# A fused transformer kernel on Trainium2: a halved first weight chunk, splits moved between the input's rows, a shorter last norm, and GpSimd's rows behind a later count

## The chip, the cores and the metric

One core of one Trainium2 chip runs the whole program. Its engines are TensorE (PE; its weight loads are shown as PEld), VectorE (DVE), ScalarE (ACT), GpSimd (POOL) and SyncE (SP, which here only issues DMAs). They run side by side and wait for each other on counting semaphores. The metric is the device time of one execution in microseconds (us). Three runs of the kernel before took 1221.53, 1223.04 and 1223.50 us, so its median is 1223.04 us.

## The reference

The input is one sequence of 256 tokens by 1024 features in float32. Three norm, attention and feed-forward (FFN) stages follow each other; all matrix products are float32.

```
h = layer_norm(x, g, b)
for l in range(2):                                   # first block
    proj = h @ w_in[l]                               # q, k, v, u
    a = diff_attention(q, k, v, lam, lam_init, subln_g[l])
    f = real(fft(fft(u, features), tokens)) per group, @ w_f[l] + b_f[l]
    h = layer_norm(ALPHA * h + concat(a, f) @ w_o[l], ln1_g[l], ln1_b[l])
    h = layer_norm(ALPHA * h + (silu(h @ w_g) * (h @ w_u)) @ w_down, ln2_g[l], ln2_b[l])
mod = silu(c) @ w_ada + b_ada                        # second block: shifts, scales, gates
u = modulate(rmsnorm(h), mod);  h += 0.5 * gate * swiglu(u)
u = modulate(rmsnorm(h), mod);  h += gate * mixer(u)   # stick-breaking attention and conv
u = modulate(rmsnorm(h), mod);  h += 0.5 * gate * swiglu(u)
return rmsnorm(h)
```

## The kernel before, in words

**Chunks.** All weights come as one stream of 184 chunks of 128 x 2048 float32 (1 MB each). SP loads chunk j into `raw[j % 3]`. ACT rounds it to the short matmul type (`w_hi`, a copy), DVE takes the rest (`w_lo = raw - w_hi`), and PE multiplies in passes: high by high, high by low, low by high. The inputs are split in the same way: ACT writes a scaled and shifted tile `x_full` from the transposed norm, and DVE makes `x_hi` and `x_lo` of it (`input_split`, eight tiles of 128 features, two instructions each).

**Order and waits.** Every engine's program is written out by hand and runs in order. The counts that matter: `hi_ready` (ACT has rounded a chunk), `lo_ready` (DVE has its rest; SP may also load that buffer again), `chunk_done` (PE is through with it), `x_ready` (input tiles split), `z_ready` (quarters of the normalised rows `z`). Before ACT rounds chunk j it waits until PE is through with chunk j - 3.

**Layers.** A layer of the first block takes 45 chunks: V0, V1, U0, U1, Q0, K0, Q1, K1, four for the output projection, 33 for the FFN. V0 and U0 use the input tiles 0 to 3, V1 and U1 the tiles 4 to 7 (`token_projection`, L466 on). Between V1 and U0 PE makes tables from `wf` and the constants `c32` (`fourier_tables`, L618) and waits there for both to land. The FFN's first two chunks, 12 and 13 of a layer, use all eight tiles each.

**A norm.** DVE adds the residual banks to `h` (L1191), takes statistics (L1178, L1181, L1184), GpSimd raises to the power of -1/2 (L349), DVE writes `z = (h - mean) * root` (L1200), PE transposes `z` (L519), ACT writes `x_full` (L837), DVE splits it. The product `h = z * gain + shift` that the next residual needs is done by GpSimd (`residual_stream`, L364 and L369, eight instructions), behind the input's split. Behind the last of the five layer norms DVE does it itself (L1469, L1473), since the next norm reads its result at once: ACT squares and sums `h` (L847), DVE and GpSimd make the root (L1217, L349) and DVE scales (L1226).

**The program's first microseconds.** SP issues four loads of `x`, then chunks 0 and 1, the constants, chunk 2. ACT's own DMA queue brings the first constants, `lp` and `wf` for both layers. GpSimd's queue brings `cp`, and once chunk 1 has landed two `gain_rows` and three `gate_rows` of 512 KB each. In the DMA rows q1 is SP's queue, q10 is ACT's, q0 is GpSimd's.

## Time and profile before

| | us |
|---|---|
| median of three runs | 1223.04 |
| the profiled execution, its own time | 1223.15 |
| its span, first to last instruction | 1221.4 |
| PE busy | 1161.7 (95%) |
| DVE busy | 869.0 (71%) |
| ACT busy | 606.9 (50%) |
| GpSimd busy | 115.8 (9%) |

What lies around the span is 1.75 us. Busy times overlap, so they don't add to the span. The timeline lists instructions in order of time, and the idle time ahead of one on its engine stands behind it in brackets with what ended it. The busy time of a matmul includes its drain, which overlaps the next one: what counts is the distance between starts.

### The profile page before, as it was taken

To read this page: it belongs to the slowest core of one execution; us is meant where nothing else is said; L and a number is where in the kernel's file an instruction comes from. 1 tells how busy PE (TensorE), PEld (TensorE's weight loads), DVE (VectorE), ACT (ScalarE), POOL (GpSimd) and SP (SyncE) were. 2 spreads that over 40 slices of the span, in tenths; PEclk is the share of its full clock that TensorE was granted. 3 is DMA by queue.
4 is the path that set the end of the run, shared out by engine and by line. 5 is a ranking of instruction groups with operands and counts; after the bars stand their busy time and mean duration, and the time that the engine had idled before them with its cause. 6 is when DMAs were issued, how large, how long until landed. Compare 5 with 4: busy or idle time off the path is not lost.

```text
span 1221.4 us, 17674 instructions
## 1 busy us (share of the span) xinstructions
PE 1161.7 (95%) x6612; PEld 998.8 (82%) x6612; DVE 869.0 (71%) x1128; ACT 606.9 (50%) x738; POOL 115.8 (9%) x99
## 2 busy tenths in 40 slices
PE   5999999999899999999969999999999998999997
PEld 4887888888687788888858888877989997888886
DVE  6486968888858586888886788877468377555555
ACT  4473644444458364444444445444695445444443
POOL 3301700000330170000010000000000000000000
PEclk9999999999999999999979999998999999999999
DMA  9612577775362257777535667753423543555540
GB/s 360 233 70 104 180 257 302 276 292 207 114 229 70 104 184 256 299 279 294 203 135 210 241 258 272 291 192 150 166 97 139 188 158 145 208 197 174 200 175 35
DMA packets 34847, 242.62 MB, mean 199 GB/s; under 512 B 3792, under 2 KB 5216, under 8 KB 8176
## 3 DMA queue, kind: packets, MB, share of 16 engines
q1 hardware_dynamic: 27792, 196.03, 43.2%
q0 software_dynamic: 5520, 45.17, 10.1%
q10 hardware_dynamic: 1488, 0.76, 0.2%
q8 instruction: 33, 0.54, 0.2%
q14 instruction: 14, 0.11, 0.0%
HBM read 240.90 MB, written 1.05 MB: 198 GB/s over the span
## 4 chain that ended last, share of the span: by engine, by line
PE 78%; DVE 11%; ACT 5%; issue 4%; DMA 1%; POOL 0%; SPq 0%; DVEq 0%; ACTq 0%
PE bank L429 38%; PE bank L462 24%; PE bank L464 12%; ACT w_hi L829 2%; DVE x_parts L1235 1%; DVE w_lo L1162 1%; DVE work L1286 1%; PE bank L608 1%; DVE small L1178 1%; DMA raw<-stream 1%; PE bank L519 1%; DVE h L1191 1%; DVE x_parts L1233 1%; DVE h L1211 1%; PE bank L585 1%
## 5 line engine op out<-in xcount | busy, mean ns | idle before, releaser
L1162 DVE TENSOR_TENSOR w_lo<-raw,w_hi 128x2048 fp32r<-128x2048 f32 x184 | 430.1, 2342 | 148.1 <-ACT w_hi L829 147.8
L462 PE MATMUL bank<-x_parts,w_hi 128*128 128x512 f32 x1408 | 499.1, 398 | 5.3 <-DVE w_lo L1162 3.3
L464 PE MATMUL bank<-x_parts,w_lo 128*128 128x256 f32 x1408 | 395.1, 281 | 0.0
L829 ACT ACTIVATE w_hi<-raw 128x2048 fp32r<-128x2048 f32 x184 | 350.7, 1907 | 47.7 <-PE bank L429 41.6
L462 PEld LDWEIGHTS bank<-x_parts,w_hi 128*128 128x128 f32 x1408 | 264.6, 188 | 72.4 <-DVE w_lo L1162 4.6
L464 PEld LDWEIGHTS bank<-x_parts,w_lo 128*128 128x128 f32 x1408 | 266.0, 189 | 1.4
L429 PE MATMUL bank<-x_parts,w_hi 128*128 128x256 f32 x832 | 153.0, 286 | 0.7 <-ACT work L1078 0.7
L429 PE MATMUL bank<-w_hi,hid_hi 128*128 128x512 f32 x352 | 139.3, 396 | 2.8 <-DVE hid_lo L1274 2.8
L429 PE MATMUL bank<-w_lo,hid_hi 128*128 128x512 f32 x352 | 139.0, 395 | 0.0
L429 PE MATMUL bank<-w_hi,hid_lo 128*128 128x512 f32 x352 | 138.8, 394 | 0.0
L429 PEld LDWEIGHTS bank<-x_parts,w_hi 128*128 128x128 f32 x832 | 129.4, 191 | 3.8 <-issue 2.0
L429 PE MATMUL bank<-x_parts,w_lo 128*128 128x256 f32 x416 | 117.6, 283 | 0.0
L1286 DVE SCALAR_TENSOR_TENSOR work<-work,c_act 128x384 f32 x168 | 104.0, 619 | 5.9
L869 ACT ACTIVATE hid_hi<-work 128x512 fp32r<-128x512 f32 x44 | 27.8, 632 | 127.7 <-PE bank L429 114.7
L853 ACT ACTIVATE work<-bank 128x512 f32<-128x512 f32 x44 | 26.3, 597 | 122.6 <-PE bank L464 122.6
L429 PEld LDWEIGHTS bank<-w_hi,hid_hi 128*128 128x128 f32 x352 | 66.0, 187 | 20.1 <-DVE hid_lo L1274 4.1
L429 PE MATMUL bank<-w_hi,x_parts 128*128 128x512 f32 x224 | 74.1, 408 | 6.4 <-DVE x_parts L1235 4.5
L429 PEld LDWEIGHTS bank<-x_parts,w_lo 128*128 128x128 f32 x416 | 79.6, 191 | 0.0
L429 PEld LDWEIGHTS bank<-w_hi,hid_lo 128*128 128x128 f32 x352 | 66.0, 187 | 16.0
L429 PEld LDWEIGHTS bank<-w_lo,hid_hi 128*128 128x128 f32 x352 | 66.0, 188 | 14.1
L1274 DVE TENSOR_TENSOR hid_lo<-work,hid_hi 128x512 fp32r<-128x512 f32 x44 | 32.7, 743 | 60.1 <-ACT hid_hi L869 60.1
L349 POOL TENSOR_TENSOR small<-small 128x1 f32<-128x1 f32 x18 | 11.6, 643 | 540.3 <-DVE small L1217 426.0
(168 smaller groups left out, 1227.8 us busy)
## 6 DMA issues: line engine op xcount, KB each, us to landing
raw<-stream SPq DMA_DIRECT2D x184, 1024.0 KB, 4.8
work<-ada POOLq DMA_DIRECT2D x24, 1536.0 KB, 7.1
gain_rows<-rows POOLq DMA_DIRECT2D x11, 512.0 KB, 4.9
gate_rows<-rows POOLq DMA_DIRECT2D x3, 512.0 KB, 11.1
h<-x SPq DMA_DIRECT2D x4, 256.0 KB, 5.0
out<-z SPq DMA_DIRECT2D x4, 256.0 KB, 2.1
c<-consts SPq DMA_DIRECT2D x1, 962.0 KB, 12.9
wf<-w_f ACTq DMA_DIRECT2D x2, 256.0 KB, 14.5
```

Of the source, the lines that this page charges most:

```text
L429: last = nc.tensor.matmul(out, stationary, moving, start=start and i == 0, stop=stop and i == 2, skip_group_check=True)
L462: nc.tensor.matmul(pair[:, n, :], wh[:, k, cols], x_parts[:, k, :, :].rearrange("p a n -> p (a n)"), start=k == 0, stop=False, skip_group_ ...
L464: last = nc.tensor.matmul(pair[:, n, 0:S], wl[:, k, cols], x_hi[:, k, :], start=False, stop=k == KT - 1, skip_group_check=True)
L519: last = nc.tensor.transpose(XT[k // 2][:, k % 2 * S + m * P:k % 2 * S + (m + 1) * P], z[:, m, k * P:(k + 1) * P], ident)
L585: last = nc.tensor.matmul(SCORES[u][:, m * S:(m + 1) * S], qT[r:r + HD, p, m * P:(m + 1) * P], kT[r:r + HD, p, :], start=True, stop=True, ...
L608: last = nc.tensor.matmul(bank[:, at:at + VD], aT_s[:, h % 2, kk, m * P:(m + 1) * P], v_s[:, kk, h * VD:(h + 1) * VD], start=kk == 0, stop ...
L829: nc.scalar.activation(w_hi[j % SLOTS][:, :], raw[j % SLOTS][:, :], ACT.Copy).then_inc(hi_ready, 1)
L853: nc.scalar.activation(gate_rest.rearrange("p (a n) -> p a n", a=2), GATE[:, :, S:2 * S], ACT.Copy)\
L869: nc.scalar.activation(out[:, :, :].rearrange("p k n -> p (k n)"), hidden, ACT.Copy)\
L1162: nc.vector.tensor_tensor(w_lo[j % SLOTS][:, :], raw[j % SLOTS][:, :], w_hi[j % SLOTS][:, :].bitcast(F32), ALU.subtract).then_inc(lo_ready, 1)
L1274: nc.vector.tensor_tensor(lo[:, :, :].rearrange("p k n -> p (k n)"), hidden, hi[:, :, :].rearrange("p k n -> p (k n)").bitcast(F32), ALU.s ...
L1286: nc.vector.scalar_tensor_tensor(acc, ada_raw[:, k, :], c_act[:, k:k + 1], acc, ALU.mult, ALU.add).then_inc(ada_step, 1)
```

## The change

- At the start SP loads chunk 0 as two halves of 1024 columns, ACT rounds and DVE subtracts each half by itself, and `wf` is loaded from SP's queue, after chunk 2 and ahead of the constants.
- In the first chunks of a layer, and of the mixer, the split of chunk 1 stands between the input tiles 0 to 3 and 4 to 7 on DVE; on ACT it does so in layer 0.
- Ahead of each FFN of the first block, DVE subtracts the first half of chunk 13 before the input's tiles and the second half after them.
- The last layer norm's rows come from two operations a quarter, `y = (h - mean) * gain` and `h = y * root + shift`, and they stand between the residual sums of rows 0 and 1.
- GpSimd's rows wait also for `lo_ready`: four chunks of the layer in the first case, chunk 14's in the second.
- PE runs 30 matmuls on a tile of ones before anything else.

```diff
 SP
-            for s in range(SLOTS):
+            sp.dma_start(raw[0][:, 0:CH // 2], stream[0, :, 0:CH // 2]).then_inc(first_half_landed, 16)
+            sp.dma_start(raw[0][:, CH // 2:], stream[0, :, CH // 2:]).then_inc(raw_landed[0], 16)
+            for s in range(1, SLOTS):
                 sp.dma_start(raw[s][:, :], stream[s]).then_inc(raw_landed[s], 16)
-                if s == 1:
-                    sp.dma_start(c32[:, TRI:], consts32[:, TRI:]).then_inc(consts_landed, 16)
+            for l in range(DEPTH):
+                sp.dma_start(wf[l][:, :, :], w_f[l].rearrange("g c d -> c g d")).then_inc(wf_landed, 16)
+            sp.dma_start(c32[:, TRI:], consts32[:, TRI:]).then_inc(consts_landed, 16)
 GpSimd
-            def residual_stream(n):
+            def residual_stream(n, chunks):
                 pool.wait_ge(gain_rows_landed, 32 * n + 32)
                 pool.wait_ge(x_ready, 8 * n + 8)
+                pool.wait_ge(lo_ready, chunks)
                 pool.wait_ge(z_ready, 4 * n + 4)
...
-                residual_stream(2 * l)
+                residual_stream(2 * l, 3 * LT * l + 4)
...
-                residual_stream(2 * l + 1)
+                residual_stream(2 * l + 1, 3 * LT * l + G0 + 3)
 PE
+            def warm_up(count):
+                pe.wait_ge(ones_ready, 1)
+                for _ in range(count):
+                    nc.tensor.matmul(B[0][:, 0:P], ones_r[:, :], ones_r[:, :], start=True, stop=True,
+                                     skip_group_check=True)
+            warm_up(30)
 ACT
                 act.dma_start(lp[l][:, :], layer_params[l]).then_inc(params_landed, 16)
-                act.dma_start(wf[l][:, :, :], w_f[l].rearrange("g c d -> c g d")).then_inc(wf_landed, 16)
...
-            split(0, 0, first=True)
-            split(0, 1, first=True)
-            act.wait_ge(params_landed, 16 * DEPTH)
+            act.wait_ge(first_half_landed, 16)
+            nc.scalar.activation(w_hi[0][:, 0:CH // 2], raw[0][:, 0:CH // 2], ACT.Copy).then_inc(first_half_hi, 1)
+            act.wait_ge(raw_landed[0], 16)
+            nc.scalar.activation(w_hi[0][:, CH // 2:], raw[0][:, CH // 2:], ACT.Copy).then_inc(hi_ready, 1)
...
+                input_full(2 * l, *columns, range(0, KT // 2))
+                if l == 0:
+                    split(t, 1, first=True)
+                input_full(2 * l, *columns, range(KT // 2, KT))
                 split(t, 2, first=l == 0)
+                act.wait_ge(params_landed, 16 * DEPTH)
                 split(t, 3)
 DVE
-                input_split(2 * l)
+                input_split(2 * l, range(0, KT // 2))
                 split(t, 1)
+                input_split(2 * l, range(KT // 2, KT))
                 split(t, 2)
                 split(t, 3)
...
+                split_half(t, 13, 0)
                 input_split(2 * l + 1)
-                split(t, 13)
+                split_half(t, 13, 1)
...
-            layer_scaled(4)
+            def last_rows(m):
+                for b in (2 * m, 2 * m + 1):
+                    nc.vector.scalar_tensor_tensor(tile_of(z, b), tile_of(h, b), moments[:, m, 0:1],
+                                                   gain_rows[:, 0, b % 2 * HALF:(b % 2 + 1) * HALF], ALU.subtract,
+                                                   ALU.mult).then_inc(y_ready, 1)
+                dve.wait_ge(inv_root_ready, 2 * 4 + m + 1)
+                for b in (2 * m, 2 * m + 1):
+                    dve.wait_ge(y_ready, b + 1)
+                    nc.vector.scalar_tensor_tensor(tile_of(h, b), tile_of(z, b), inv_root[:, m:m + 1],
+                                                   gain_rows[:, 1, b % 2 * HALF:(b % 2 + 1) * HALF], ALU.mult,
+                                                   ALU.add).then_inc(h_ready, 1)
...
+            layer_residual(4, LAYER_CHUNKS * DEPTH, (0, 1))
+            last_rows(0)
+            layer_residual(4, LAYER_CHUNKS * DEPTH, (2, 3))
+            last_rows(1)
```

The order of instructions at three places, of before and of the change. First SP's queue from the program's start; `h<-x` are the four loads of the input, `raw0` to `raw2` the chunk buffers, `c32` the constants. Before:

```order
L318 DMA h<-x 128x512 x4
L322 DMA raw0<-stream 128x2048
L322 DMA raw1<-stream 128x2048
L324 DMA c32<-consts32 128x1924
L322 DMA raw2<-stream 128x2048
```

With the change:

```order
L321 DMA h<-x 128x512 x4
L324 DMA raw0<-stream 128x1024
L325 DMA raw0<-stream 128x1024
L327 DMA raw1<-stream 128x2048
L327 DMA raw2<-stream 128x2048
L329 DMA wf0<-w_f 128x4x128
L329 DMA wf1<-w_f 128x4x128
L330 DMA c32<-consts32 128x1924
```

The constants have moved from third among the big loads to last, behind chunk 2 and both `wf`, which came from ACT's queue; chunk 3, the next load, stays behind all of them.

Second, DVE at the input of layer 0 (the same in layer 1), around the split of chunk 1, `w_lo1<-raw1,w_hi1`. Before, the last of eight input tiles and what follows it:

```order
L1233 CAST x_parts<-x_full 128x256 [waits x_full_ready]
L1235 TENSOR_TENSOR x_parts<-x_full,x_parts 128x256 [waits x_hi_ready]
L1162 TENSOR_TENSOR w_lo1<-raw1,w_hi1 128x2048 [waits hi_ready]
L1162 TENSOR_TENSOR w_lo2<-raw2,w_hi2 128x2048 [waits hi_ready]
L1162 TENSOR_TENSOR w_lo0<-raw0,w_hi0 128x2048 [waits hi_ready]
```

With the change, the fourth tile, the chunk and the fifth tile:

```order
L1262 CAST x_parts<-x_full 128x256 [waits x_full_ready]
L1264 TENSOR_TENSOR x_parts<-x_full,x_parts 128x256 [waits x_hi_ready]
L1182 TENSOR_TENSOR w_lo1<-raw1,w_hi1 128x2048 [waits hi_ready]
L1262 CAST x_parts<-x_full 128x256 [waits x_full_ready]
L1264 TENSOR_TENSOR x_parts<-x_full,x_parts 128x256 [waits x_hi_ready]
```

Chunk 1 has moved ahead of eight of the sixteen instructions of the input.

Third, DVE behind the last layer norm, from the statistics of rows 0's second half on. Before:

```order
L1181 BN_AGGR small<-small 128x2 [waits bn_done]
L1184 TENSOR_SCALAR small<-small 128x1 [waits moments_ready]
L1200 TENSOR_SCALAR z<-h,small 128x512 [waits inv_root_ready] x4
L1469 TENSOR_TENSOR h<-z,gain_rows 128x512 [waits z_ready,gain_rows_landed]
L1469 TENSOR_TENSOR h<-z,gain_rows 128x512 [waits z_ready] x3
L1473 TENSOR_TENSOR h<-h,gain_rows 128x512 [waits h_scaled] x4
L1217 TENSOR_SCALAR small<-small 128x1 [waits squares_done]
```

With the change:

```order
L1213 TENSOR_SCALAR small<-small 128x1 [waits moments_ready]
L1506 SCALAR_TENSOR_TENSOR z<-h,small,gain_rows 128x512 x2
L1512 SCALAR_TENSOR_TENSOR h<-z,small,gain_rows 128x512 [waits y_ready,inv_root_ready]
L1512 SCALAR_TENSOR_TENSOR h<-z,small,gain_rows 128x512 [waits y_ready]
L1220 SCALAR_TENSOR_TENSOR h<-h,bank 128x512 [waits res_bank,h_ready]
L1207 BN_STATS small<-h 128x6 [waits summed]
```

Twelve instructions on quarters of `h` have become eight, four for each row block; those of block 0 stand ahead of the residual sums of block 1.

## Rows read from the trace of the kernel before

**Rows 1.** The page, part 4: the chain that ended last, shares by engine.
```profile
PE 78%; DVE 11%; ACT 5%; issue 4%; DMA 1%; POOL 0%; SPq 0%; DVEq 0%; ACTq 0%
```

**Rows 2.** Windows: stretch, length, busy us (count) of PE, PEld, DVE, ACT, POOL, clock, DMA, GB/s.
```profile
18.00:21.00 3.00, 3.00 (x8) 2.32 (x9) 2.86 (x10) 2.90 (x6) 0.00 (x0) 1.00 1.02 409
125.00:312.00 187.00, 184.77 (x963) 155.88 (x963) 150.52 (x156) 90.33 (x83) 26.49 (x18) 1.00 0.67 253
617.00:636.00 19.00, 9.27 (x58) 8.35 (x57) 16.43 (x37) 4.25 (x12) 3.68 (x6) 0.65 0.25 78
```

**Rows 3.** Timeline of layer 0's input: start, us, engine, instruction [idle before, releaser].
```profile
8.64 0.69 DVE L1178 BATCH_NORM_STATS2 small<-h 128x6 f32<-128x512 f32 x1 [0.26 <-DMA h<-x]
...
9.73 2.08 DVE L1200 TENSOR_SCALAR z<-h,small 128x512 f32<-128x512 f32 x4
...
11.78 1.91 ACT L829 ACTIVATE w_hi<-raw 128x2048 fp32r<-128x2048 f32 x1 [5.30 <-DMA raw<-stream]
13.72 2.29 DVE L1162 TENSOR_TENSOR w_lo<-raw,w_hi 128x2048 fp32r<-128x2048 f32 x1 [1.91 <-ACT w_hi L829]
14.50 1.91 ACT L829 ACTIVATE w_hi<-raw 128x2048 fp32r<-128x2048 f32 x1 [0.81 <-DMA raw<-stream]
...
16.32 3.98 ACT L837 ACTIVATE x_full<-bank,cp 128x256 f32<-128x256 f32 x8
...
17.80 0.77 PE L429 MATMUL bank<-w_hi,x_parts 128*128 128x512 f32 x1 [3.72 <-DVE x_parts L1235]
...
25.57 1.92 ACT L829 ACTIVATE w_hi<-raw 128x2048 fp32r<-128x2048 f32 x1 [3.47 <-PE bank L429]
...
29.92 1.30 DVE L1351 TENSOR_TENSOR work<-lp 128x64 f32<-128x64 f32 x1
...
30.75 1.88 PE L618 MATMUL bank<-wf,c 128*128 128x512 f32 x4
...
43.59 1.09 ACT L940 ACTIVATE work<-bank 128x512 f32<-128x512 f32 x2 [3.46 <-PE bank L429]
```

**Rows 4.** DMA queues from 17 to 20 us: packets, MB, share of 16 engines.
```profile
DMA packets 342, 1.23 MB, mean 409 GB/s; under 512 B 35, under 2 KB 137, under 8 KB 260
...
q1 hardware_dynamic: 98, 0.67, 54.4%
q0 software_dynamic: 128, 0.50, 41.8%
q10 hardware_dynamic: 116, 0.05, 6.4%
```

**Rows 5.** Line L923, the two loads of wf: from issue to landing.
```profile
DMA to landing us min/median/max: 7.9/14.5/21.1
```

**Rows 6.** Timeline of layer 1's input.
```profile
327.59 8.88 DVE L1162 TENSOR_TENSOR w_lo<-raw,w_hi 128x2048 fp32r<-128x2048 f32 x3
...
329.93 0.50 PE L429 MATMUL bank<-w_hi,x_parts 128*128 128x512 f32 x1 [1.05 <-DVE w_lo L1162]
```

**Rows 7.** Timeline of the input of layer 0's FFN, and of layer 1's (last row).
```profile
123.50 0.29 DVE L1233 CAST x_parts<-x_full 128x256 fp32r<-128x256 f32 x1 [1.35 <-ACT x_full L837]
...
128.82 5.58 DVE L1162 TENSOR_TENSOR w_lo<-raw,w_hi 128x2048 fp32r<-128x2048 f32 x2
...
131.16 0.50 PE L462 MATMUL bank<-x_parts,w_hi 128*128 128x512 f32 x1 [0.87 <-DVE w_lo L1162]
...
435.80 0.51 PE L462 MATMUL bank<-x_parts,w_hi 128*128 128x512 f32 x1 [0.87 <-DVE w_lo L1162]
```

**Rows 8.** Timeline of the last layer norm's rows on DVE.
```profile
623.61 2.07 DVE L1200 TENSOR_SCALAR z<-h,small 128x512 f32<-128x512 f32 x4
...
625.60 2.49 DVE L1469 TENSOR_TENSOR h<-z,gain_rows 128x512 f32<-128x512 f32 x4
...
628.00 2.49 DVE L1473 TENSOR_TENSOR h<-h,gain_rows 128x512 f32<-128x512 f32 x4
```

**Rows 9.** Timeline of DVE's last instructions.
```profile
1216.05 1.42 DVE L1621 SCALAR_TENSOR_TENSOR z<-h,small,gain_rows 128x512 f32<-128x512 f32 x2
```

More of the change, by code:

```diff
@@ L198, in fused_blocks @@
         common_landed = sem("common_landed")
+        first_half_landed = sem("first_half_landed")
+        first_half_hi = sem("first_half_hi")
         x_landed = [sem(f"x_landed{b}") for b in range(4)]
@@ L225, in fused_blocks @@
         inv_root_ready = sem("inv_root_ready")
+        y_ready = sem("y_ready")
         z_ready = sem("z_ready")
@@ L516, in transposes @@
                     m, c = b // 2, b % 2
-                    pe.wait_ge(z_ready, 4 * n + b + 1)
+                    pe.wait_ge(z_ready, 4 * back(n) + b + 1)
                     for k in range(4 * c, 4 * c + 4):
@@ L829, in split, with input_full @@
                 nc.scalar.activation(w_hi[j % SLOTS][:, :], raw[j % SLOTS][:, :], ACT.Copy).then_inc(hi_ready, 1)
-            def input_full(n, gain, shift):
-                for k in range(KT):
+            def input_full(n, gain, shift, ks=range(KT)):
+                for k in ks:
                     act.wait_ge(transposed, 4 * back(n) + k // 2 + 1)
@@ L1002, in _ @@
                 if l == 0:
-                    input_full(0, lambda k: cp[:, LNI_G + k:LNI_G + k + 1], lambda k: cp[:, LNI_B + k:LNI_B + k + 1])
+                    columns = (lambda k: cp[:, LNI_G + k:LNI_G + k + 1], lambda k: cp[:, LNI_B + k:LNI_B + k + 1])
                 else:
-                    input_full(2 * l, *layer_columns(l - 1, LN2_G, LN2_B))
+                    columns = layer_columns(l - 1, LN2_G, LN2_B)
+                    split(t, 1)
+                input_full(2 * l, *columns, range(0, KT // 2))
+                if l == 0:
+                    split(t, 1, first=True)
+                input_full(2 * l, *columns, range(KT // 2, KT))
                 split(t, 2, first=l == 0)
+                act.wait_ge(params_landed, 16 * DEPTH)
                 split(t, 3)
@@ L1163, in split, with split_half @@
                                         w_hi[j % SLOTS][:, :].bitcast(F32), ALU.subtract).then_inc(lo_ready, 1)
+            def split_half(t, j, part):
+                cols = slice(part * (CH // 2), (part + 1) * (CH // 2))
+                dve.wait_ge(hi_ready, 3 * t + (j + 1))
+                last = nc.vector.tensor_tensor(w_lo[j % SLOTS][:, cols], raw[j % SLOTS][:, cols],
+                                               w_hi[j % SLOTS][:, cols].bitcast(F32), ALU.subtract)
+                if part == 1:
+                    last.then_inc(lo_ready, 1)
             def tile_of(buffer, b):
@@ L1185, in layer_stats, with layer_residual @@
                         .then_inc(spread_ready, 1)
-            def layer_residual(n, chunks):
+            def layer_residual(n, chunks, banks=range(4)):
                 dve.wait_ge(h_ready, 4 * n)
-                for b in range(4):
+                for b in banks:
                     bank_summed(n, b, chunks)
@@ L1227, in rms_scaled, with input_split @@
                                             ALU.mult, ALU.mult).then_inc(z_ready, 1)
-            def input_split(n):
-                for k in range(KT):
+            def input_split(n, ks=range(KT)):
+                for k in ks:
                     at = 8 * back(n) + k + 1
@@ L1332, in _ @@
                 layer_stats(0, b)
-            dve.wait_ge(common_landed, 16)
-            dve.wait_ge(c_act_ready, 1)
             for l in range(DEPTH):
@@ L1340, in _ @@
                 if l == 0:
-                    split(0, 0)
+                    dve.wait_ge(first_half_hi, 1)
+                    nc.vector.tensor_tensor(w_lo[0][:, 0:CH // 2], raw[0][:, 0:CH // 2],
+                                            w_hi[0][:, 0:CH // 2].bitcast(F32), ALU.subtract)
+                    dve.wait_ge(hi_ready, 1)
+                    nc.vector.tensor_tensor(w_lo[0][:, CH // 2:], raw[0][:, CH // 2:],
+                                            w_hi[0][:, CH // 2:].bitcast(F32), ALU.subtract).then_inc(lo_ready, 1)
                 else:
                     keep_shifts(l - 1)
-                input_split(2 * l)
+                input_split(2 * l, range(0, KT // 2))
                 split(t, 1)
+                input_split(2 * l, range(KT // 2, KT))
                 split(t, 2)
                 split(t, 3)
+                dve.wait_ge(common_landed, 16)
+                dve.wait_ge(c_act_ready, 1)
                 dve.wait_ge(params_landed, 16 * DEPTH)
@@ L1484, in _ @@
             keep_shifts(2)
-            input_split(6)
+            input_split(6, range(0, KT // 2))
             split(MIX_T, 1)
+            input_split(6, range(KT // 2, KT))
             t = MIX_T
```

14 lines of the change are left out of this document (3 added, 11 removed).

## The prediction, made before the changed kernel was run

> **What bounds the kernel now.** I read the chain that ended last first: PE holds 78% of it [rows 1], and inside an FFN, from 125 to 312 us, PE is busy 184.8 of 187.0 us [rows 2]. So time is to be had only where PE waits or runs at the lower clock: at the joints, where a norm hands over to the next input. Then I read the timeline at those joints, and at the start the DMA queues. The reader should see four things. At the start PE's first product begins at 17.80 us [rows 3]: chunk 0 was landed at 11.7, chunk 1 at 14.5, and ACT, in order, rounds both before it turns to the input at 16.32. Ahead of layer 1's second chunk PE waits 1.05 us for DVE's `w_lo` [rows 6]. Ahead of each FFN's second chunk it waits 0.87 us for the same [rows 7]. And behind the last layer norm DVE's three passes over four quarters hold everything up [rows 8].
>
> **The start.** Durations from rows 3: a rounding of 1.91 us halves to 0.96, a subtraction of 2.29 to 1.15. The eight input tiles take 5.3 us on DVE (123.50 to 128.82 [rows 7]), 0.66 each. A chunk on PE takes 5.45 us: chunks 2 and 3 lie between 32.63 (30.75 + 1.88) and 43.6.
>
> Step 1, DMA. `wf` is 1024 packets of 512 B. A packet of ACT's queue costs 26 ns of one engine (6.4% of 48 engine-us by 116 [rows 4]). The two loads landed 7.9 and 21.1 us after their issue [rows 5], so I estimate that some 430 of the packets had gone when `x` was complete and 640 when chunk 0 was: 0.7 and 1.0 us over 16 engines. Without them `x` is complete at 7.9 us, chunk 0 at 10.7, its first half (0.52 MB at 0.41 MB a us [rows 4]) at 9.5, chunk 1 at 13.4.
>
> Step 2, ACT and DVE. `z` is done at 11.81 - 0.7 = 11.1. ACT rounds the halves by 10.5 and 11.7 and goes on to the input. DVE subtracts from 11.1 to 13.4, splits the first tile by 14.1, and PE starts at 14.1, 3.7 us sooner. Chunk 1, now behind ACT's first four tiles, is rounded by about 15.7; DVE has four tiles by 16.0, chunk 1 by 18.3, tiles 4 to 7 by 21.0. PE asks for chunk 1 at 19.6 and then for a tile every 1.4 us: no wait. Before, chunk 0 lasted 7.7 us (17.80 to 25.5), because matmuls stood 0.375 us apart (8 in 3.00 us [rows 2], against 0.23 at the full rate), although the record of the granted clock says 1.00 there. With the full clock PE is through chunk 1 at 25.0.
>
> Step 3, what that meets. Then come the Fourier tables, which want `wf` and the constants. These now stand behind chunk 2 in SP's queue, and chunk 3 behind them, while GpSimd's five loads of 512 KB run beside (issued once chunk 1 is landed, as before). From 17 to 20 us the three queues got 98, 128 and 116 packets, nearly one for one, whatever their size [rows 4]. So the 64 small packets an engine of `wf` each wait for one of GpSimd's 40 of 4 KB, which cost 157 ns (41.8% of 48 by 128). Chunk 2 lands at 15.9 (13.4 + 1.05 MB at 0.41); then 40 x 157 + 64 x 26 ns = 8.0 us to 23.9; the constants (0.98 MB) 26.3; chunk 3 28.9. PE waits 1.3 us for the constants, makes the tables by 28.2 and has chunk 2 by 33.7. Chunk 3 is rounded and subtracted by 33.1, in time; PE is through it at 39.1. But ACT now waits, behind chunk 3, for DVE's lambda (1.3 us [rows 3] and about 0.4 behind it), copies V (1.0, two of the pair at 43.59), rounds chunk 4 (1.9), and DVE subtracts beside GpSimd (2.5, my estimate between 2.29 and the 2.79 of rows 7): 40.2. PE starts chunk 4 at 40.3 instead of 43.6. **Gain 3.3 us**: PE's own path was worth more, 5.9 (3.7 and 2.2 of clock). All later work of the layer shifts with it. The ends I keep: 5.9 if the transfers keep up, 1.0 if chunk 3 lands 2.3 us later still.
>
> In the Trainium skill, "DMA: Bandwidth & Descriptors", section "Queues, rings and completion order", a DMA engine goes round its queues packet by packet, not byte by byte. By it `wf` is a bad neighbour for GpSimd's rows, as worked out above; the counts of rows 4 agree. Were bytes shared evenly, `wf` and the constants (1.5 MB at 0.2) would be landed at 23.3, there would be no wait at the tables, and the start would give about 4.
>
> The 30 warm-up matmuls (128 x 128, short type, on ones) are in no row. From the nearest, 0.375 us for 512 columns at the lower rate, I bound one between a quarter of that and all of it: 2.8 to 11.3 us from 1.1 us on, so the end is at 3.9 to 12.4. `z`'s first quarter is there at 9.0, so the late end delays the transposes by up to 3.4 us and PE's start by perhaps 2; an early end leaves some 5 us of idleness in which the clock can fall again, and chunk 0 costs up to 2.2 more. Either way PE is through chunk 1 by 27.2 and loses at most 0.9 to the wait above. I take 0.
>
> **Layer 1's input.** DVE takes chunk 1 behind four tiles: ready at 327.59 - 2.65 + 2.29 = 327.2, while PE is through chunk 0 at 328.7; tile 4 is split at 327.9. The wait of 1.05 us goes, with the slower first matmul behind it (0.16): **1.2 us**. Next late would be chunk 2, subtracted by 332.2, wanted at 334.2. The mixer's input has the same new order, but no wait of this kind.
>
> **The two FFN inputs.** Half of chunk 13 (1.15 us) fits into the 1.35 us that DVE idles ahead of the first tile [rows 7]; the other half ends at 128.9 + 1.15 = 130.0, when PE wants it at 130.1. 0.87 + 0.16 each, **2.1 us** for two. If the half ran into the tiles, that would cost 0.2 a stage at most.
>
> **The last layer norm.** Before, DVE needs 6.9 us (623.61 to 630.49 [rows 8]) for twelve passes. Now eight operations of one kind, a tensor with a column and a tensor; nearest, two of these in 1.42 us [rows 9], 0.71 each: 5.7. The root is hidden behind the first two of each block. **1.2 us**, 0.9 to 1.5. ACT's squares of block 1 follow as before, and so does the rest.
>
> **GpSimd's rows later.** They start about 3.3 us later behind an FFN's input and 7 us later behind layer 1's. Beside them DVE's subtraction took 2.79 instead of 2.29 us [rows 7], so this spares the two behind the input and slows others, where DVE idles 1 to 4 us before it. They are wanted 70 us or more later. 0, either way.
>
> **Sum.** 3.3 + 1.2 + 2.1 + 1.2 = 7.8 us off the profiled execution's own 1223.15: 1215.3. The median of the runs is 0.1 lower, which I ignore.
>
> **Rivals.**
> A, the transfers keep up. Against it stand the DMA rates, full at 409 GB/s in rows 4. The start then gives 5.9, less what the chain from chunk 3 takes, nothing if it lands by 25.5: 1212.7.
> B, PE's start is held: the warm-up runs late, or half the clock, and the transfers are late too: the start gives 1.5, 1217.2.
> C, slower: the stream is starved. GpSimd's rows and `wf` hold back chunk 3, in order before every later chunk; ACT waits for it and with it the evacuation of V, so PE stands still. Each us that chunk 3 lands behind 28.9 costs one. The four gains of 7.8 are used up at 36.7; at 39 the time is 1225.5. Against it: all bytes until then, at the rate of rows 4, are through by about 34.
> D, the gains at the joints don't come, since PE finds another wait right behind each (ACT's rounding of the next chunk): only the start is left, 1219.9.
>
> **Chances.** The forecast 0.50, A 0.22, B 0.16, D 0.08, C 0.04. The range for 8 in 10 goes from A's side (1212.2) to B's with chunk 3 2 us later still (1219.0); outside lie D, C and the rims of A and B. A measurement of this kernel tells a change from none at about 0.2%, 2.4 us. Slower by more than that is half of C and no more, 0.02; within it the rest of C and a small part of D, 0.04; faster 0.94.
>
> **What would show it.** PE's first product on chunk 0 at about 14.1 us, its matmuls 0.23 us apart. A PE wait of about 1.3 us for a DMA ahead of the tables, near 25 us; none would mean A. PE's chunk 4 at about 40.3, behind DVE's `w_lo`. No wait of PE at the second chunk of layer 1 and of the two FFNs. From the last layer norm's last statistics to the next scaling 1.2 us less. PE's first product later than 17.8, or the third wait of the start above 5 us, would make the prediction wrong; so would any new PE wait of several us behind 50 us.

## The result and the profile after

The changed kernel took 1212.05 us, median of 4 runs (1210.70 to 1214.21), beside 1222.28 us for the kernel before on the same chip (1221.49 to 1223.50): ratio 0.9917, 95% interval 0.9897 to 0.9937. The forecast was 1215.3 and its range ended at 1212.2, so the range missed the time. Rival A's time was 1212.7. The first of these runs is the profiled one: 1210.7, span 1209.0 against 1221.4 before. One run of the kernel before, in a later set, took 1632.09 us at a granted clock of 0.65 and is left out of the ratios.

The chain of waits, shares by engine, stands as in [rows 1]; TensorE has more of it, VectorE less:

```profile
PE 80%; DVE 10%; ACT 5%; issue 4%; DMA 0%; POOL 0%; DVEq 0%; SPq 0%; ACTq 0%
```

The start of the changed kernel, by its timeline, answers to [rows 3] (`...` stands for rows left out):

```profile
1.17 6.66 PE L585 MATMUL bank<-ones_r 128*128 128x128 f32 x30 [1.17 <-POOL ones_r L399]
...
10.86 1.22 DVE L1369 TENSOR_TENSOR w_lo<-raw,w_hi 128x1024 fp32r<-128x1024 f32 x1
12.00 1.22 DVE L1372 TENSOR_TENSOR w_lo<-raw,w_hi 128x1024 fp32r<-128x1024 f32 x1
...
14.03 0.47 PE L437 MATMUL bank<-w_hi,x_parts 128*128 128x512 f32 x1 [0.81 <-DVE x_parts L1264]
15.88 2.28 DVE L1182 TENSOR_TENSOR w_lo<-raw,w_hi 128x2048 fp32r<-128x2048 f32 x1
...
24.29 1.91 ACT L845 ACTIVATE w_hi<-raw 128x2048 fp32r<-128x2048 f32 x1 [4.96 <-DMA raw<-stream]
25.01 1.88 PE L634 MATMUL bank<-wf,c 128*128 128x512 f32 x4
...
31.97 2.75 DVE L1182 TENSOR_TENSOR w_lo<-raw,w_hi 128x2048 fp32r<-128x2048 f32 x1 [2.50 <-ACT w_hi L845]
```

The first product begins at 14.03 and the tables at 25.01, without an idle time in brackets: the forecast had 14.1 and 25.0, but then a wait. Chunk 3 is rounded from 24.29 (forecast landing 28.9), chunk 4 is subtracted by 34.7 (forecast 40.2), three us before TensorE wants it at 37.7. By the windows, TensorE ran at full pace; the row answers to the first of [rows 2]:

```profile
18.00:21.00 3.00, 3.00 (x15) 2.49 (x14) 2.86 (x10) 1.33 (x1) 0.00 (x0) 1.00 1.04 426
```

The DMA queues from 15 to 17 us and from 17 to 20 (packets, MB, share), and the two loads' time from issue to landing, answer to [rows 4, 5]:

```profile
q1 hardware_dynamic: 731, 0.71, 119.8%
...
q1 hardware_dynamic: 124, 0.85, 67.7%
q0 software_dynamic: 98, 0.40, 33.5%
...
c<-consts SPq DMA_DIRECT2D x1, 962.0 KB, 14.0
wf<-w_f SPq DMA_DIRECT2D x2, 256.0 KB, 11.5
```

`wf` stands in the first row: 731 packets of SP's queue in 2 us, 654 of them `wf`'s of 512 B, and not one of GpSimd's (q0) beside them. The other 370 of `wf`'s 1024 went from 13 to 15 us, also without any of q0. GpSimd's first packets come between 17.5 and 18 us, and by 17 `wf` is through. The constants, issued at 6.44, landed 14.0 later, at 20.4 instead of 26.3.

Later joints, by the timeline; they answer to [rows 6 to 8]:

```profile
116.02 1.22 DVE L1189 TENSOR_TENSOR w_lo<-raw,w_hi 128x1024 fp32r<-128x1024 f32 x1
117.15 0.28 DVE L1262 CAST x_parts<-x_full 128x256 fp32r<-128x256 f32 x1
118.05 0.77 PE L470 MATMUL bank<-x_parts,w_hi 128*128 128x512 f32 x1 [0.53 <-DVE x_parts L1264]
...
316.16 0.77 PE L437 MATMUL bank<-w_hi,x_parts 128*128 128x512 f32 x1 [0.26 <-DVE x_parts L1264]
...
420.91 0.47 PE L470 MATMUL bank<-x_parts,w_hi 128*128 128x512 f32 x1 [1.23 <-DVE x_parts L1264]
...
611.01 1.41 DVE L1506 SCALAR_TENSOR_TENSOR z<-h,small,gain_rows 128x512 f32<-128x512 f32 x2
612.33 1.41 DVE L1512 SCALAR_TENSOR_TENSOR h<-z,small,gain_rows 128x512 f32<-128x512 f32 x2
...
620.79 3.68 PE L527 MATMUL bank<-c,z 128*128 128x128 f32 x16 [7.91 <-DVE z L1255]
```

Behind these, no row of TensorE waits for `w_lo` at the second chunk: the waits of 1.05 and 0.87 twice are gone. But the first product of layer 0's FFN now takes 0.77 us where it took 0.47 before, and layer 1's first product 0.77 where it took 0.47.

**Where the time went, by stage.** The cuts are starts of TensorE's rows: the first attention scores, the first long FFN-down row of layer 0 in the chain of waits (24 matmuls, 5.59 us), the first product of layer 1's FFN, the same x24 row there, the first product behind the last norm, and the mixer's first row on 256 columns that waits for ACT (847.71 before, 835.03 after). Lengths in us, of profiled executions; the four columns on the right are explained below.

| stretch | before | changed | changed, again | start alone | all but the start | start, kept busy |
|---|---|---|---|---|---|---|
| to the first scores | 56.44 | 50.70 | 50.98 | 52.70 | 56.89 | 50.91 |
| attention 0, FFN 0's input | 91.64 | 90.37 | 92.04 | 92.16 | 91.94 | 90.98 |
| FFN 0, layer 1's input, attention 1 | 280.96 | 279.84 | 279.26 | 280.28 | 279.24 | 280.34 |
| FFN 1's input | 24.00 | 22.60 | 24.97 | 23.97 | 23.03 | 23.99 |
| FFN 1, last norm | 182.77 | 181.27 | 181.27 | 182.77 | 181.25 | 182.76 |
| next FFN, mixer's input | 211.90 | 210.25 | 210.24 | 211.90 | 210.71 | 209.94 |
| mixer, last FFN | 373.69 | 373.97 | 374.04 | 373.72 | 375.14 | 374.28 |
| span | 1221.4 | 1209.0 | 1212.8 | 1217.5 | 1218.2 | 1213.2 |

The 12.4 us of the profiled executions are 5.74 + 1.27 + 1.12 + 1.40 + 1.50 + 1.65 - 0.28.

### The profile page after: what moved, and what is told of

It reads as the page before. It is cut to its first block, busy times and chain, and to the rows that moved or that the text cites. A ratio compares the mean times of both kernels' runs of the same rounds, so it can differ in the third digit from the quotient of the medians.

```text
span 1209.0 us, 17742 instructions
## 1 busy us (share of the span) xinstructions
PE 1164.8 (96%) x6642; PEld 1003.4 (83%) x6642; DVE 864.5 (72%) x1127; ACT 607.7 (50%) x739; POOL 105.1 (9%) x99
## 3 DMA queue, kind: packets, MB, share of 16 engines
HBM read 240.90 MB, written 1.05 MB: 200 GB/s over the span
## 4 chain that ended last, share of the span: by engine, by line
PE 80%; DVE 10%; ACT 5%; issue 4%; DMA 0%; POOL 0%; DVEq 0%; SPq 0%; ACTq 0%
PE bank L437 38%; PE bank L470 25%; PE bank L472 13%; ACT w_hi L845 2%; DVE work L1315 1%; DVE small L1207 1%; PE bank L624 1%; DVE h L1220 1%; DVE w_lo L1182 1%; PE bank L527 1%; DVE x_parts L1264 1%; DVE h L1240 1%; DVE z L1236 1%; PE bank L601 1%; PE bank L614 1%
## 5 line engine op out<-in xcount | busy, mean ns | idle before, releaser
L1182 DVE TENSOR_TENSOR w_lo<-raw,w_hi 128x2048 fp32r<-128x2048 f32 x181 | 421.3, 2330 | 144.7 <-ACT w_hi L845 144.6
L869 ACT ACTIVATE work<-bank 128x512 f32<-128x512 f32 x44 | 26.3, 597 | 122.1 <-PE bank L472 122.1
L437 PEld LDWEIGHTS bank<-w_lo,hid_hi 128*128 128x128 f32 x352 | 66.0, 188 | 14.1
L437 PE MATMUL bank<-w_hi,x_parts 128*128 128x512 f32 x224 | 71.6, 396 | 2.3 <-DVE x_parts L1264 1.5
```

What stands on the lines that cost most here:

```text
L437: last = nc.tensor.matmul(out, stationary, moving, start=start and i == 0, stop=stop and i == 2, skip_group_check=True)
L869: nc.scalar.activation(gate_rest.rearrange("p (a n) -> p a n", a=2), GATE[:, :, S:2 * S], ACT.Copy)\
L1182: nc.vector.tensor_tensor(w_lo[j % SLOTS][:, :], raw[j % SLOTS][:, :], w_hi[j % SLOTS][:, :].bitcast(F32), ALU.subtract).then_inc(lo_ready, 1)
```

## The experiments

Diffs are against the changed kernel. Each time is a median, with the ratio to the kernel before on the same chip. Full pace means matmuls of 512 columns 0.23 us apart, half pace about 0.4.

**The changed kernel once more.** No edit.

> The changed kernel once more, to see what varies from one execution to the next. Theory (the clock at the joints is granted anew in each execution): the order and the waits are the same (no wait for the tables, first product of TensorE at 14.0 to 14.5 us, chunk 3 landed by 24.5), but the first products may take 0.77 us a pair instead of 0.47, and then tables come 2 us later; median 1210.7 to 1214.5. Rival (the early start brings the full clock each time): first products at full pace again and time within 0.5 us of 1210.7.

Measured: 1214.45 us (1213.42 to 1216.02, 5 runs), 0.9938 [0.9924, 0.9951]. The first product again at full pace, no wait at the tables: the start gave 5.46. But both FFN inputs cost 0.40 and 0.97 more than before (by the table), though no `w_lo` wait came back. The windows, of the first execution and of this one, show why (stretch, busy times, then clock):

```profile
115.00:123.00 8.00, 7.47 (x40) 6.25 (x39) 7.65 (x21) 5.88 (x9) 0.06 (x1) 0.79 0.00 0
418.00:426.00 8.00, 6.77 (x43) 5.74 (x42) 7.72 (x20) 5.89 (x9) 0.00 (x0) 1.00 0.00 0
```

```profile
115.00:123.00 8.00, 7.29 (x31) 5.97 (x32) 7.65 (x21) 5.88 (x9) 0.37 (x1) 0.59 0.00 0
418.00:426.00 8.00, 6.57 (x27) 5.43 (x28) 7.65 (x21) 5.30 (x9) 0.87 (x1) 0.64 0.00 0
```

TensorE is busy about as long, but gets 31 and 27 matmuls through instead of 40 and 43: the granted clock was 0.59 and 0.64, most of the stretch at its lower level, 1.2 GHz, instead of 0.79 and 1.00, the last all at 2.4 GHz. The stretches don't begin at the same work (the first product of layer 1's FFN is at 420.91 and at 422.28); counted over 6 us from the first product on, it is 21 and 22 matmuls instead of 31 and 33. The same program, the same order. The nine runs of the changed kernel have a median of 1214.2, and that lies inside the forecast range.

**The parts: the start alone, and all but the start.** The first keeps the old order at layer 1's and the FFNs' inputs, the old norm, and GpSimd's residual products (`h = z * gain + shift`) as early as before. The mixer's input keeps the new order in it:

```diff
-                pool.wait_ge(lo_ready, chunks)
-                split_half(t, 13, 0)
...
-                split_half(t, 13, 1)
+                split(t, 13)
...
-            last_rows(0)
+            for b in range(4):
+                nc.vector.tensor_tensor(tile_of(h, b), tile_of(z, b), gain_rows[...], ALU.mult)
```

> The change's start alone (halves of chunk 0, wf on SP's queue, chunk 1 between the input's halves in layer 0, 30 warm-up matmuls); the last norm, GpSimd's rows, chunk 13 and layer 1's order as in the kernel before. Theory 1 (the terms add, and the start is worth what PE's own path lost): first score matmuls (32x256, x16) at 50.8 us as in the changed kernel, 5.7 us less than before, time 1216.6. Theory 2 (the start was worth 3.3 as predicted, and the rest of the 10 us is the clock or the later stages): 1218.9 and the first scores at 53.2.

The second has the old start (whole chunk 0, the old order of loads and of layer 0's input, `wf` on ACT's queue, no warm-up) and all else of the change:

```diff
-            sp.dma_start(raw[0][:, 0:CH // 2], stream[0, :, 0:CH // 2]).then_inc(first_half_landed, 16)
-            for l in range(DEPTH):
-                sp.dma_start(wf[l][:, :, :], ...).then_inc(wf_landed, 16)
-            warm_up(30)
```

> The changed kernel with the whole start put back to the kernel before (first scores again at 56.5 us); last norm, GpSimd's rows, chunk 13 and layer 1's order stay changed. Theory 1 (terms add, the joints are worth what was predicted, 1.2 + 2.1 + 1.2 = 4.5 us): 1217.8. Theory 2 (the joints are worth the 6.7 us that the two profiled executions show behind the first scores): 1215.6.

Measured: the start alone 1218.46 (1214.54 to 1219.20, 6 runs), 0.9957 [0.9945, 0.9969]; all but the start 1219.67 (1218.37 to 1220.72, 7 runs), 0.9975 [0.9964, 0.9986]. The two differences, 4.4 and 3.2, make 7.6; the whole change's over both sets of runs is about 8.2. By the table the start alone gave 3.74, the rest's sum of stages is 3.2, less than either expectation (4.5 and 6.7). The start alone lost 2 us to the whole change in one place, its first products:

```profile
14.25 0.77 PE L436 MATMUL bank<-w_hi,x_parts 128*128 128x512 f32 x1 [0.81 <-DVE x_parts L1263]
14.81 0.63 PE L436 MATMUL bank<-w_lo,x_parts 128*128 128x512 f32 x1
```

These begin 0.56 us apart and the next ones 0.43, though the record of the granted clock there is 1.00, as it was before.

**GpSimd's loads early: the meeting that Step 3 worked out.** `gain_rows` and `gate_rows` are issued at 10.0 instead of 13.2.

```diff
-            pool.wait_ge(raw_landed[1], 16)
```

> The changed kernel with GpSimd's loads of gain and gate rows issued as soon as the two roots are done (about 10 us), not behind chunk 1. It makes the collision that the prediction reckoned with: these 4 KB packets then move while the 64 small packets an engine of wf do. Theory 1 (packets alternate between queues, so wf is slowed to the pace of the rows): constants landed at 24 to 25 us instead of 20.4, chunk 3 at 27 to 28 instead of 24.2, DVE's w_lo of chunk 4 at 37.5 to 38.5 and first scores up to 1.2 us later, time 0.5 to 1.2 us slower. Theory 2 (bytes are shared and nothing of it is on the path): constants by 22.5, first scores unchanged at 50.8.

> The changed kernel with GpSimd's gain rows issued ahead of chunk 2's landing, once more. Theory of the prediction's Step 3 (wf and GpSimd's rows share the engines packet for packet): constants land 19 to 20 us after issue, at 26.1, and chunk 3 at 28.7; if TensorE's first products run at full pace this time it is ready for the tables at 25.3 and must wait 0.5 to 1 us for the constants, a row of idle time that the changed kernel does not have; time 1 us above the changed kernel's. Rival (the late constants don't hold TensorE): no idle time at the tables, time equal to the changed kernel's within 0.5 us.

Measured: 1213.42 (1213.12 to 1215.04, 4 runs), 0.9929 [0.9915, 0.9943], and again 1215.08 (1213.16 to 1215.87, 5 runs), 0.9936 [0.9922, 0.9949]. Of the first, the queues from 17 to 20 us and the two loads' times to landing, and then, from the timeline, the tables and chunk 3 on ACT:

```profile
q0 software_dynamic: 283, 1.03, 88.2%
q1 hardware_dynamic: 281, 0.14, 16.4%
...
c<-consts SPq DMA_DIRECT2D x1, 962.0 KB, 19.5
wf<-w_f SPq DMA_DIRECT2D x2, 256.0 KB, 17.6
```

```profile
27.65 1.88 PE L633 MATMUL bank<-wf,c 128*128 128x512 f32 x4
28.66 1.91 ACT L844 ACTIVATE w_hi<-raw 128x2048 fp32r<-128x2048 f32 x1 [9.11 <-DMA raw<-stream]
```

Now the packets go one for one, 283 to 281. The constants, issued at 6.57, land at 26.1 (Step 3: 26.3), chunk 3 at 28.6 (Step 3: 28.9); chunk 4 is subtracted by 39.1 (Step 3: 40.2). So the arithmetic was right for two queues that meet, and the rule of the Trainium skill, "DMA: Bandwidth & Descriptors", section "Queues, rings and completion order", holds in these counts: packet by packet, not byte by byte (a packet of that page can hold several descriptors; what is counted here are the packets of the profile). In the changed kernel the two don't meet: the rows are issued at 13.15 and their first packets come after 17.5. But TensorE ran its first products at half pace here, in both runs, and was ready for the tables only at 27.65; the wait itself could not show.

To show it, matmuls of ones that nothing reads were added ahead of TensorE's first products, in this kernel:

```diff
             warm_up(30)
+            fill(8)
...
                 transposes(2 * l)
+                if l == 0:
+                    fill(4)
```

> GpSimd's rows early, and TensorE kept busy at the start: 8 more matmuls of ones ahead of its transposes and 4 between these and its first product. Theory of Step 3 (with wf and the rows one for one the constants land at 26 us, later than TensorE needs them if it runs at full pace): first product near 14.5, chunks 0 and 1 done by 25.5, an idle time of 0.6 to 1.2 us at the tables with a DMA or GpSimd's or SP's transfer as releaser, then another near chunk 4 (DVE's w_lo ready at 39.1, wanted at 38.9) of under 0.5; first scores at 52 to 52.5. Rival 1 (the pace stays half whatever TensorE does there, so the wait stays hidden): no idle time, first scores at 52.7 to 53.3. Rival 2 (full pace and the late constants still don't hold): first scores at 51.0 to 51.3.

Measured: 1215.14 (1215.02 to 1216.10, 5 runs), 0.9945 [0.9932, 0.9959]. The load of the constants with its time to landing, and the timeline of TensorE and of its weight loads (PEld):

```profile
c<-consts SPq DMA_DIRECT2D x1, 962.0 KB, 20.8
```

```profile
14.33 0.77 PE L436 MATMUL bank<-w_hi,x_parts 128*128 128x512 f32 x1 [0.27 <-DVE x_parts L1272]
...
27.02 0.39 PE L436 MATMUL bank<-w_hi,x_parts 128*128 128x512 f32 x1
27.48 0.30 PEld L640 LDWEIGHTS bank<-wf,c 128*128 128x128 f32 x2 [0.50 <-DMA c<-consts]
27.48 1.98 PE L640 MATMUL bank<-wf,c 128*128 128x512 f32 x4
...
40.58 0.47 PE L436 MATMUL bank<-x_parts,w_hi 128*128 128x256 f32 x2 [0.22 <-DVE w_lo L1190]
```

The pace stayed half, as rival 1 had it. Yet here, where the constants land latest, at 27.4, the weight load of the tables waits 0.50 us for them, by name, so that the tables stand 0.46 us behind the product before them instead of 0.23. Chunk 4 has the wait for `w_lo` that Step 3 had put there, 0.22 us, at 40.58 (forecast 40.3). So both waits of Step 3 exist once the two queues meet. With TensorE 2.4 us earlier, as in the changed kernel, they would have been longer; their full size is an inference, since no run had late constants and full pace together.

**What sets the pace of the first products?** The start alone once more, then with the same 12 added matmuls, and the changed kernel with them as control.

> The start of the change alone, once more: first chunk in halves, wf on SP's queue and GpSimd's rows later, with layer 1's and the FFNs' inputs and the last norm as before. Theory (whether TensorE's first products run at full pace differs from execution to execution): its first product comes at 14.0 to 14.6 again, and if it runs at full pace this time, tables come at 25.0 to 25.7 and the time is 2 us below the other run's 1218.5, about 1216.5. Rival (something of the rest of the change sets the clock at the start): first products at 0.77 us again, tables at 27 or later, 1218 to 1219.

> The start of the change alone, with the same 12 more matmuls of ones. Theory (half pace in the first products is TensorE's answer to its idle 2 us and 0.8 us ahead of them): first products at 0.47 us, tables at 25.2 to 25.5 instead of 27.1, time 1.7 us below the 1218.5 to 1218.8 of the start alone, about 1217. Rival (the pace there belongs to something else in the kernel): 0.77 us again, tables at 27, 1218.5.

> The changed kernel with the same 12 more matmuls of ones. Theory (its first products run at full pace already): first product at 14.1 to 14.5 at 0.47 us, tables at 25.0 to 25.5, time within 1 us of the changed kernel's 1212 to 1214.5. Rival (the matmuls hold the first product up): 0.5 to 1 us later at every stage, 1213 to 1215.5.

(GpSimd's residual products stand as before in the start alone; the first of these three texts says otherwise by mistake.)

Measured: 1218.82 (1216.42 to 1219.32), 0.9964 [0.9950, 0.9977]; kept busy 1215.00 (1214.91 to 1216.52), 0.9945 [0.9931, 0.9958]; control 1213.41 (1211.85 to 1214.72), 0.9931 [0.9918, 0.9945]; 5 runs each. The first ran at half pace again. Kept busy, the start alone ran at full pace:

```profile
13.09 1.09 PE L583 MATMUL bank<-ones_r 128*128 128x128 f32 x4
14.26 0.47 PE L436 MATMUL bank<-w_hi,x_parts 128*128 128x512 f32 x1
```

Its median lies 3.5 and 3.8 us below those of the two sets without the added matmuls, of which the table has 1.8 at the start. So idleness ahead of the products seems to have a part in it, by one profile and five times. It can't be all: the changed kernel runs at full pace with 0.81 us of it, the kernel with GpSimd's loads early and the same added matmuls at half pace with 0.27.

**No warm-up.**

```diff
-            warm_up(30)
```

> The changed kernel without the 30 warm-up matmuls. Theory 1 (the warm-up ends at about 7.5 us and the 16 transposes from 9.6 us on raise the clock by themselves): PE's first product at 14.0 us with its matmuls 0.23 us apart, first scores at 50.8, time within 0.3 us of the changed kernel. Theory 2 (the warm-up is what gives the full clock at 14 us): matmuls 0.43 us apart up to about 17 us, first scores at 52 to 52.8, 1.3 to 2 us slower.

Measured: 1214.73 (1213.19 to 1215.59, 4 runs), 0.9935 [0.9921, 0.9950]. First product at 14.48, at full pace, so no gain of the 30 matmuls is shown: the time lies within the changed kernel's own runs.

**`wf` back on ACT's queue.**

```diff
-                sp.dma_start(wf[l][:, :, :], ...).then_inc(wf_landed, 16)
+                act.dma_start(wf[l][:, :, :], ...).then_inc(wf_landed, 16)
```

> The changed kernel with wf's loads back on ACT's queue behind chunk 1's splits, where they stood before the change. Theory (wf ahead of the constants clears the queue before the rows come): wf would now be issued near 11 us and share the engines with the rows and chunks 2 and 3 and the constants; the constants on SP's queue land earlier (issue near 4.9, landing before 18), wf at 20 to 25, so tables may wait for wf; time from equal to 1 us above the changed kernel's. Rival (the order of the two has no price): within 0.3 us, no idle time at the tables.

Measured: 1213.83 (1213.67 to 1217.24, 5 runs), 0.9937 [0.9923, 0.9950]. No idle time at the tables, the rival's case. What I expected was wrong in two points: `wf` was issued at 1.81 and 2.85, as before the change, and not near 11, and the constants came 14.6 us after issue, at 19.8. The first product began at 14.85, 0.6 to 0.8 later than in the two profiles of the changed kernel, with 184 packets of ACT's queue beside 184 of SP's from 10 to 13 us; Step 1 had worked out 0.7 to 1.0 for `wf` ahead. It ran at half pace, so that the first scores came 2.4 us later than in the changed kernel; by the median of its runs that isn't seen.

**The last norm in its old form.**

```diff
-            last_rows(0)
+            for b in range(4):
+                nc.vector.tensor_tensor(tile_of(h, b), tile_of(z, b), gain_rows[...], ALU.mult)
```

> The changed kernel with the last norm's rows in their old form (tiles in the order of before, scale and shift as two passes over four tiles) . Theory (term of 1.2 us as forecast, 1.5 as the two traces differ): TensorE idles 9.4 us instead of 7.9 ahead of the last norm's transposes, and the time is 1.2 to 1.6 us above the changed kernel's, 1213.3 to 1213.8. Rival (GpSimd's and VectorE's other work there hides it): within 0.3 us of the changed kernel.

Measured: 1215.81 (1213.53 to 1218.60, 6 runs), 0.9947 [0.9935, 0.9959], 1.4 above the changed kernel on the same chip, with overlapping ranges. TensorE's idle time ahead of the transposes:

```profile
623.16 3.68 PE L527 MATMUL bank<-c,z 128*128 128x128 f32 x16 [9.43 <-DVE z L1255]
```

9.43 against 7.91. The table's stretch with the last norm was 182.76 or 182.77 in all five profiles with the old norm, 181.25 to 181.27 in eleven of the twelve with the new (the twelfth has 40 matmuls added ahead of the transposes, see below): 1.50 us, the one term that stands clear in every profile.

**FFN's second chunk in one piece.**

```diff
-                split_half(t, 13, 0)
...
-                split_half(t, 13, 1)
+                split(t, 13)
```

> The changed kernel with the FFN's second chunk (chunk 13) split in one piece behind all eight tiles of the input instead of in two halves between them. Theory (half a split between the tiles keeps VectorE off the path): nothing gained or lost by more than 0.9 us in all; if the wait of 0.87 us in front of chunk 13's products comes back at both layers, 1.7 us above the changed kernel (1213.8). Rival (the half between the tiles costs the input its own time, 1.2 us a half at two layers): 1 to 2 us below the changed kernel, 1210.0 to 1211.0.

Measured: 1215.80 (1213.50 to 1218.64, 6 runs), 0.9948 [0.9935, 0.9960], 1.35 above the changed kernel on the same chip, with overlapping ranges. At layer 0:

```profile
118.37 0.76 PE L470 MATMUL bank<-x_parts,w_hi 128*128 128x512 f32 x1 [0.26 <-DVE x_parts L1264]
...
125.13 0.49 PE L470 MATMUL bank<-x_parts,w_hi 128*128 128x512 f32 x1 [0.55 <-DVE w_lo L1182]
```

A wait of 0.55 is back; the first products at half pace hide the rest of it. At layer 1, at half pace too, no wait came back, but the stage took 23.67, as with the whole chunk elsewhere. What the half in front costs the input is read from the start of TensorE's transposes to its first product, over both layers of all profiles: with the whole chunk 3.05 us where the transposes run at full pace (2.19 us) and up to 3.93 where they don't, with halves 3.41 or 3.42 in 19 of 24 cases and 3.53 to 3.93 in five with slow transposes. So the half costs 0.37, more than the 0.2 at most that I had put, but only where the transposes are fast; here, at layer 0, it was 3.42 against 3.38.

**Busy joints.** Added are matmuls of ones that nothing reads: 42 at the start, then 8 (layer 1's input), 12 (each FFN's), 36 (last norm), 4 (mixer's input) and 8 (last FFN's); in the second kernel 30, 14, 22, 40, 8 and 16.

```diff
+                keep_warm(12)
                 transposes(2 * l + 1)
```

> Adds matmuls of ones, without a reader, where TensorE waits for a normed tile: 42 instead of 30 at the start, 8 ahead of layer 1's input, 12 ahead of each layer's FFN input, 36 ahead of the last norm's transposes, 4 and 8 in the mixer. Theory (what the change left on the table at the joints is the clock after the idle stretch): the first products behind each joint run at full pace (0.47 instead of 0.77 us), 1.5 to 2 us a joint at up to four joints, 1205 to 1209. Rival (the clock follows something that these small matmuls don't feed, or they hold the transposes up): 1211 to 1214 with the same granted clock in the stretches behind the joints.

> As warm_joints but with 30 matmuls at the start and more at the joints, to close the idle stretch wholly where 12 left 1.5 us: 14 ahead of layer 1's input, 22 ahead of the FFNs' inputs, 40 ahead of the last norm's, 8 and 16 in the mixer. Theory (TensorE's clock falls at the joints because it idles there): with no idle stretch left the granted clock in 115 to 123 us and 418 to 426 us is 1.00 and the time is 1 us or more below warm_joints' 1212.3. Rival (the clock falls there in some executions whatever runs, and the added matmuls at the lower clock hold up the transposes): 1212 to 1215.

Measured: 1212.28 (1211.75 to 1214.86, 5 runs), 0.9926 [0.9913, 0.9939], and 1214.74 (1212.84 to 1216.92, 5 runs), 0.9940 [0.9926, 0.9953]. By the windows of the second the clock at both FFN inputs is full:

```profile
115.00:123.00 8.00, 6.57 (x41) 5.52 (x42) 7.65 (x21) 5.89 (x9) 0.64 (x1) 1.00 0.00 0
418.00:426.00 8.00, 6.40 (x44) 5.39 (x44) 7.65 (x21) 4.86 (x9) 0.87 (x1) 1.00 0.00 0
```

So keeping TensorE busy goes with the full clock there, in this one profile of it; the kernel with the old norm had first products of 0.47 us at both without it. The first version's 1205 to 1209 was missed. But ahead of layer 1's input and of the last norm the matmuls end after `z` is ready and hold the transposes: layer 1's start 172.9 us behind layer 0's long FFN-down row instead of 171.2, and the stretch of 181.27 takes 182.65. Together they are not faster than the changed kernel beyond the spread; neither version is shown to beat it.

## Why the prediction was wrong, step by step

- **Steps 1 and 2 were right.** First product 14.03 (14.1), through chunk 1 at 25.01 (25.0), matmuls 0.23 us apart. This path gave 5.74 of the 5.9 it was worth.
- **Step 3 failed.** It put a wait of 1.3 us for the constants and a late chunk 4 on the path. It let "the 64 small packets an engine of `wf` each wait for one of GpSimd's". That needs both queues full at once. All 1024 packets of `wf` were through by 17 us, alone, and GpSimd's first came behind, after 17.5. So there was no wait for the constants (20.4, not 26.3), chunk 3 stood ready 4.6 us earlier, chunk 4 was no limit, and the start gave 5.74 instead of 3.3. This is rival A by its sign, "none would mean A", though not for its reason: transfers ran at full rate, as forecast, but in another order. The profile of before could have shown it: its rows were issued once chunk 1 had landed, at 14.77, and all 128 q0 packets of the window from 17 to 20 us [rows 4] lie behind 18. I carried their issue over and left out the 3.2 us or more between issue and first packet. With the loads issued 3.1 us earlier the queues did meet, and the constants landed at 26.1: the arithmetic was right, its premise was not.
- **Layer 1's input** (1.2): 1.12 in the profiled execution, 1.70 in the next. Right as far as is known: it was not tried alone. The stretch that holds it took 280.28 to 281.11 in the four profiles with the old order and 278.88 to 280.03 in twelve with the new; a thirteenth, with 14 matmuls added ahead of the transposes, took 281.18.
- **The two FFN inputs** (2.1): both waits went, as said. Gains 1.27 and 1.40 once, -0.40 and -0.97 the other time. The term counted the wait and no clock; the first matmuls behind the joint take 0.47 or 0.77 us as the granted clock has it, and that can move more time than the wait. All profiles together bear the term out better than these two. From the FFN's first product to its long down row, layer 1 took 23.67 to 24.00 in the five with a whole chunk, and with halves 22.60 to 23.03 in eleven of twelve, 24.97 in one; layer 0 took 23.67 to 23.98 with a whole chunk, and with halves 22.76 to 23.40 in nine, 24.61 to 25.02 in three. Up to 0.37 of that gain is lost ahead of the first product (see the whole chunk above). The wait had also hidden short stretches of the lower clock: where the start alone was kept busy, layer 1's first product took 0.77 us, the wait behind it was 0.25 instead of 0.87, and the stage took 23.99 all the same. With the wait gone, a low clock there costs its full time.
- **The last norm** (1.2): 1.50. Under-sized by 0.3: the four operations of a block take 2.73 us (611.01 to 613.74), 0.68 each instead of 0.71. That is 0.24 for eight.
- **GpSimd's residual products later** (0): not tried alone; open. The stages of the changed kernel show no loss but 0.3 us in the last, and that one took 373.69 to 375.14 in the profiles of the table.
- **Not in the sum**: the mixer's input, 1.65. All of it lies behind the mixer's first product, 0.76 us before (834.23) and 0.47 after (823.20): the granted clock in the next 3 us was 0.50 before and 1.00 after. Only the kernel before has the old order there. The start alone has the new one, and its three profiles had 211.90, as before, 210.18 (again: 632.07 to 842.25) and 209.94 (kept busy). So these runs show no merit of the edit in it.
- **The warm-up** (0): no gain shown, as taken.
- Rival D is refuted by the gone waits, B and C by the start. Of the 4.6 us between forecast and profiled execution (12.4 against 7.8), 2.4 are Step 3's, 1.65 the mixer's clock, 0.5 the small terms. That the four runs' median fell 0.15 us below the range, while the five of the next set lie inside it, is luck; that Step 3's waits never came, in either profile, is not.

What stays open: why the start alone, the kernels with GpSimd's loads early and the one with `wf` on ACT's queue ran their first products at half pace in every profile and the changed kernel did not, at a granted clock of 1.00 in all of them.

## What to carry to other kernels

A transfer meets another only if both queues have packets then: before pricing contention, read from the trace when each queue's first packet comes, not when it was issued. Behind a joint, price the wait and the clock apart: where TensorE had idled 2.8 us and another 0.5 to 0.7, the same program got 31 or 21 matmuls through in the next 6 us. And take one more set of runs before a difference of 2 us is explained; here two sets of one kernel gave 1212.05 and 1214.45.

## What the runs showed of the hardware that I had not expected

GpSimd's queue takes long to start. Loads issued at 13.15 had no packet before 17.5 us and 18 by 18 us; issued at 14.77, in the kernel before, none before 18 and 2 by 18.25; issued at 10.02, in the kernel with them early, none before 13.5 and 9 by 14:

```profile
13.15 1.11 POOL L360 DMA_DIRECT2D gain_rows<-rows  x2 [3.24 <-DMA raw<-stream]
```

The issue of the constants behind `wf`'s 1024 packets held SP 5.81 us. In the kernel before it took 0.45, with `wf` back on ACT's queue 0.63:

```profile
6.44 5.81 SPq L330 DMA_DIRECT2D c<-consts  x1
```

A packet of 512 B costs an engine about as much alone as beside another queue's larger ones. From 13 to 15 us 390 small packets, 370 of them `wf`'s, and 69 of 8 KB took 99.4% of 32 engine-us; at 310 ns for one of 8 KB (156 with 16 tiny ones took 100.8% of 48 from 10 to 13 us) that leaves some 27 ns for a small one, my estimate. Against GpSimd's, 281 cost 16.4% of 48 engine-us, 28 ns. The row from 15 to 17 us must not be divided by its 731 packets: 49 of them are the constants', of 7.7 KB.
